# Two bank reads ahead of the last lower half, and one lower half made by GpSimd in place of VectorE

## The chip, the cores and the metric

The kernel runs on one core of a Trainium2 chip. The metric is the device time of one execution in microseconds (us), as a median of several runs. The core has five engines with queues of their own that meet only at semaphores: TensorE (PE in the profile, its weight loads PEld), VectorE (DVE), ScalarE (ACT), GpSimd (POOL) and SyncE (SP), which issues the loads.

## The reference

Two transformer-like blocks on one sequence of 512 tokens, width 1024, all in float32. The change touches only the feed-forward part of the first block:

```python
h = rmsnorm(x, norm_ffn[l])
x = x + jnp.square(jax.nn.relu(h @ w_ff1[l])) @ w_ff2[l]   # 1024 -> 4096 -> 1024
```

## The kernel before

Each float32 operand of TensorE is split into an upper half (rounded to fp32r by ScalarE, `w_hi`, `f_hi`) and a lower half (the remainder, `w_lo`, `f_lo`). A product is then three matmuls: upper by upper, upper by lower and lower by upper. Weights come through a ring of four slots in `raw`, `w_hi` and `w_lo`, each 128 x 1024; a slot is a panel.

The feed-forward part runs in four quarters of the hidden width (`ffn(i)`, 1024 hidden columns each). A quarter has eight dense panels (`h @ w_ff1`), and then four **pairs** (`pair(i, c)`, c = 0 to 3), which multiply the squared activations by `w_ff2`. A pair makes two output tiles of 128 rows by 512 tokens with seven products in place of eight (Strassen's scheme in Winograd's form). The seven are called p1 to p7. Each is one **turn** of TensorE: twelve matmuls of 256 columns into one half of a bank. The first pair of a quarter takes the turns in the order p1, p5, p2, p6, p3, p7, p4 (`FIRST_PAIR`), the others in the order p1, p2, p6, p5, p7, p3, p4 (`NEXT_PAIR`).

The weights of a pair fill the four slots. Slot 0 is a loaded panel, used by p1 and p2. Slots 1 and 2 hold four sums and differences of the loaded panels (`ss`), which VectorE makes (`first` to `fourth` in `weight_sums`); p6 and p5 use the halves of slot 1, p7 and p3 those of slot 2. Slot 3 is half a loaded panel, for p4. ScalarE makes the upper halves of slots 0 to 3 in this order (`pair_upper`). Before the change the lower halves are made as follows:

- slot 0 by GpSimd, four pieces of 128 x 256 (`pair_lower`, through the helper at L830);
- slot 1 by VectorE, two instructions of 128 x 512 (`lower(0)` for p6, `lower(1)` for p5, L2466), counted by `sum_lo_dve`;
- slot 2 by GpSimd, four pieces, counted by `sum_lo_pool`;
- slot 3 by GpSimd, two pieces.

GpSimd goes through the pairs in this order. A pair's p1 needs all of slot 0, its upper half and its lower half (`panel_split`).

After a turn VectorE adds its bank to `xT` (a **bank read**, L2557 or, for the first p1, L2519). A later turn in the same bank half goes on from what stands there, so it must wait until the earlier one has been read. Turns wait for reads by the count of `chain`, five per pair (`read(n)`). In the first pair p3 waits for the read of p5, and p7 for that of p6. VectorE is also forming the activations of the last hidden tile then (`forms(7)`, with `f_lo` for the lower halves, the newest of them at L2510).

In the last quarter ScalarE and VectorE also begin the two normalizations that follow: `scale_upper`, `scale_lower`, the squares (`both_squares(e)`, L1808 and L1809) and their sums (`add_squares(e)`, into `hf`).

## Time and profile before

| | |
|---|---|
| median of 3 runs | 1632.52 us (1631.73 to 1632.7) |
| the profiled execution: its own time | 1632.63 us |
| its span, first to last instruction | 1630.9 us |
| TensorE busy | 1603.0 us, 98% |
| GpSimd busy in the four pairs of the second quarter | 36.48 of 40.13 us |
| VectorE busy in the same stretch | 29.92 of 40.13 us |

The profile is of one execution. Its span is 1.7 us shorter than the execution's own time, which includes what lies before the first and after the last instruction. Busy shares over the whole span say little here, since the pairs take 40 us in each of four quarters. In a row of the timeline the columns are the start and the length in us, engine, line, operation, output and inputs, and in brackets the idle time before it with what ended it.

### The profile page before, as it was taken

Reading aid. Unit: us, or ns where it says so; the run is one execution under the profiler, and the core shown is the slowest. Engines: PE = TensorE matmul, PEld = TensorE weight load, DVE = VectorE, ACT = ScalarE, POOL = GpSimd, SP = SyncE. Lnnn points to the kernel's source line nnn. Section 1 sums busy time; section 2 is a strip of 40 time slices with the busy share of each in tenths; the row PEclk is TensorE's granted clock in tenths of the full one; section 3 lists DMA queues with packets and bytes.
Section 4 is the critical chain, followed back from the end, with each engine's and each line's share of the span. In section 5 each row is a group of like instructions: output and inputs, shape, how many; then the busy total and the mean of one; then the engine's idle time right before and its main releaser. Section 6 shows DMA issues by size and latency. Waiting matters only on the chain.

```text
span 1630.9 us, 23121 instructions
## 1 busy us (share of the span) xinstructions
PE 1603.0 (98%) x8079; PEld 1349.4 (83%) x8079; DVE 1001.6 (61%) x1563; ACT 874.9 (54%) x1189; POOL 777.2 (48%) x966
## 2 busy tenths in 40 slices
PE   7999999999999999999999999999999999999998
PEld 6888888888888898989897788888888887888886
DVE  3466666631114676758587957447447548688677
ACT  6467777753234544444466645444444446755675
POOL 7453333346656495867679535635635633000000
PEclk9999999999999999999999999999999999999999
DMA  7222221123333233242424222422422423332321
GB/s 210 78 79 63 64 77 58 46 65 116 91 109 98 78 95 112 78 116 79 128 65 118 76 66 78 116 65 78 116 65 66 116 64 93 92 93 68 107 63 62
DMA packets 249053, 143.00 MB, mean 88 GB/s; under 512 B 6161, under 2 KB 245522, under 8 KB 248978
## 3 DMA queue, kind: packets, MB, share of 16 engines
q1 hardware_dynamic: 248978, 142.00, 30.4%
q8 instruction: 46, 0.75, 0.2%
q14 instruction: 29, 0.24, 0.0%
HBM read 139.89 MB, written 2.10 MB: 87 GB/s over the span
## 4 chain that ended last, share of the span: by engine, by line
PE 75%; DVE 2%; issue 1%; POOL 1%; ACT 0%; DVEq 0%
PE bank L897 17%; PE bank L898 17%; PE bank L905 17%; PE bank L1163 3%; PE bank L1168 2%; PE bank L1166 2%; PE bank L888 1%; PE bank L890 1%; PE bank L889 1%; PE bank L1291 1%; PE bank L1272 1%; PE bank L1274 1%; PE bank L1273 1%; PE bank L1417 1%; PE bank L1418 1%
## 5 line engine op out<-in xcount | busy, mean ns | idle before, releaser
L830 POOL TENSOR_TENSOR w_lo<-raw,w_hi 128x256 fp32r<-128x256 f32 x864 | 704.9, 849 | 551.9 <-ACT w_hi L1524 521.3
L897 PE MATMUL bank<-h_hi,w_hi 128*128 128x512 f32 x1252 | 497.1, 397 | 0.0
L898 PE MATMUL bank<-h_lo,w_hi 128*128 128x512 f32 x1252 | 487.9, 390 | 0.0
L1524 ACT ACTIVATE w_hi<-raw 128x1024 fp32r<-128x1024 f32 x232 | 243.5, 1054 | 317.5 <-PE bank L905 263.8
L905 PE MATMUL bank<-h_hi,w_lo 128*128 128x512 f32 x1252 | 309.8, 389 | 0.0
L897 PEld LDWEIGHTS bank<-h_hi,w_hi 128*128 128x128 f32 x1252 | 235.1, 188 | 54.1 <-issue 6.0
L898 PEld LDWEIGHTS bank<-h_lo,w_hi 128*128 128x128 f32 x1252 | 235.1, 188 | 52.0 <-issue 4.1
L905 PEld LDWEIGHTS bank<-h_hi,w_lo 128*128 128x128 f32 x1252 | 235.0, 188 | 49.2 <-issue 0.5
L1163 PE MATMUL bank<-f_hi,w_hi 128*128 128x256 f32 x448 | 127.7, 285 | 6.4 <-DVE xT L2557 5.3
L1166 PE MATMUL bank<-f_lo,w_hi 128*128 128x256 f32 x448 | 126.7, 283 | 0.0
L1168 PE MATMUL bank<-f_hi,w_lo 128*128 128x256 f32 x448 | 126.7, 283 | 0.0
L2421 DVE TENSOR_TENSOR xT<-xT,bank 128x512 f32<-128x512 f32 x70 | 45.5, 684 | 88.1 <-PE bank L905 53.2
L1163 PEld LDWEIGHTS bank<-f_hi,w_hi 128*128 128x128 f32 x448 | 85.8, 192 | 8.3 <-issue 8.0
L1166 PEld LDWEIGHTS bank<-f_lo,w_hi 128*128 128x128 f32 x448 | 85.9, 192 | 0.2
L1168 PEld LDWEIGHTS bank<-f_hi,w_lo 128*128 128x128 f32 x448 | 85.9, 192 | 0.0
L830 POOL TENSOR_TENSOR w_lo<-ss,w_hi 128x256 fp32r<-128x256 f32 x64 | 61.7, 994 | 31.6 <-ACT w_hi L1753 31.3
L2405 DVE TENSOR_TENSOR gated<-sg,bank 128x512 f32<-128x512 f32 x16 | 11.0, 688 | 104.6 <-PE bank L905 104.3
L2557 DVE TENSOR_TENSOR xT<-xT,bank 128x256 f32<-128x256 f32 x112 | 46.3, 419 | 38.8 <-PE bank L1168 37.8
L2871 DVE TENSOR_TENSOR w_lo<-raw,w_hi 128x1024 fp32r<-128x1024 f32 x40 | 48.6, 1217 | 0.0
L1624 ACT ACTIVATE ee<-ee 128x512 f32<-128x512 f32 (+1 forms) x56 | 33.6, 613 | 27.8 <-DVE ee L2276 22.2
L1029 PE MATMUL bank<-qk 128*128 128x64 f32 (+1 forms) x384 | 42.4, 265 | 0.0
L1029 PEld LDWEIGHTS bank<-qk 128*128 128x128 f32 (+1 forms) x384 | 41.7, 183 | 0.8 <-DVE hf L2366 0.3
(465 smaller groups left out, 2852.5 us busy)
## 6 DMA issues: line engine op xcount, KB each, us to landing
raw<-in_w_ff SPq DMA_DIRECT2D x64, 512.0 KB, 4.1
raw<-in_w_in SPq DMA_DIRECT2D x56, 512.0 KB, 3.7
raw<-in_m_w_in SPq DMA_DIRECT2D x48, 512.0 KB, 3.9
raw<-in_r_w_in SPq DMA_DIRECT2D x24, 512.0 KB, 3.9
raw<-in_m_w_out SPq DMA_DIRECT2D x16, 512.0 KB, 3.4
raw<-in_r_w_out SPq DMA_DIRECT2D x16, 384.0 KB, 3.1
raw<-in_w_up_b SPq DMA_DIRECT2D x8, 512.0 KB, 4.1
raw<-in_w_out SPq DMA_DIRECT2D x8, 512.0 KB, 4.1
```

Source lines behind the costliest of these rows:

```text
L830: return pool.tensor_tensor(w_lo[:, s, part], full, w_hi[:, s, part].bitcast(F32), ALU.subtract)
L897: pe.matmul(dst, w_hi[:, s, c], hi[:, k, :], start=(k == 0), stop=False)
L898: pe.matmul(dst, w_hi[:, s, c], lo[:, k, :], start=False, stop=False)
L905: mm = pe.matmul(dst, w_lo[:, s, c], hi[:, k, :], start=False, stop=(k == kt - 1))
L1029: mm = pe.matmul(dst.rearrange("p (b t) -> p b t", t=h), qk[:, m - 2, c], right, start=True, stop=True, skip_group_check=True)
L1163: pe.matmul(dst, w_hi[:, s, at], f_hi[:, form, k, :], start=(k == 0 and (name in ("p1", "p2", "p5") or r == 2)), stop=False, skip_group_ch ...
L1166: pe.matmul(dst, w_hi[:, s, at], f_lo[:, form, k, :], start=False, stop=False, skip_group_check=True)
L1168: mm = pe.matmul(dst, w_lo[:, s, at], f_hi[:, form, k, :], start=False, stop=(k == NC - 1), skip_group_check=True)
L1524: act.activation(w_hi[:, p % RING, :], raw[:, p % RING, :], ACT.Copy).then_inc(hi_ready[p % RING], 1)
L2421: dve.tensor_tensor(xT[:, j, :], xT[:, j, :], bank[t % RING][:], ALU.add).then_inc(taken[t % RING], 1)
L2557: ins = dve.tensor_tensor(x, x, src[:, left], op)
L2871: dve.tensor_tensor(w_lo[:, q, :], raw[:, q, :], w_hi[:, q, :].bitcast(F32), ALU.subtract).then_inc(lo_ready[q], 1)
```

## The change

Three things change, all in the pairs.

1. The lower half of slot 1 that p5 uses is made by GpSimd, in two pieces of 128 x 256 between slot 0 and slot 2, and no more by VectorE. `sum_lo_pool` counts three to a pair instead of two, `sum_lo_dve` one.
2. In the first pair of a quarter VectorE reads the bank of p5 (`second_read`) ahead of the newest activation's last lower half, and reads p6 ahead of p2. The counts that p7 and p4 wait for follow.
3. In the last quarter ScalarE squares tiles 2 and 3 after the third pair and not after the second, and tile 4 after the fourth and not after the third.

```diff
@@ pair_lower (GpSimd)
                 ins.then_inc(lo_ready[one], 1)
+                pool.wait_ge(sum_hi, i * (2 * NC) + (2 * c + 1))
+                for q in range(2):
+                    part = slice(S + q * QP, S + (q + 1) * QP)
+                    ins = lower(1, part, ss[:, c % 2, 1, q * QP:(q + 1) * QP])
+                ins.then_inc(sum_lo_pool, 1)
                 pool.wait_ge(sum_hi, i * (2 * NC) + (2 * c + 2))
@@ pair (TensorE)
...
                     elif name == "p5":
                         bank_ready(t + 2, i, F_N)
-                        pe.wait_ge(sum_lo_dve, i * (2 * NC) + (2 * c + 2))
+                        pe.wait_ge(sum_lo_pool, i * (3 * NC) + (3 * c + 1))
                     elif name == "p7":
-                        pe.wait_ge(sum_lo_pool, i * (2 * NC) + (2 * c + 1))
-                        read(3 if c else 4)
+                        pe.wait_ge(sum_lo_pool, i * (3 * NC) + (3 * c + 2))
+                        read(3)
...
                     elif name == "p4":
                         panel_split(pe, p + 1, i, F_N)
-                        read(5 if c else 3)
+                        read(5 if c else 4)
@@ ffn (ScalarE)
-                        for e in [(0, 1), (2, 3), (4,), (5, 6, 7)][c]:
+                        for e in [(0, 1), (), (2, 3), (4, 5, 6, 7)][c]:
                             both_squares(e)
@@ forms (VectorE)
                            .then_inc(ft_made, 1)
+                        if c == NC - 1:
+                            second_read()
                         dve.wait_ge(fthi_made, i * (3 * NC) + (3 * c + 3))
...
+                def second_read():
+                    dve.wait_ge(turn_done, i * (FORMS * NC) + turn_at(0, "p5"))
+                    dve.tensor_tensor(xT[:, 1, HALF:S], xT[:, 1, HALF:S], bank[2][:, 0:HALF], ALU.add)\
                        .then_inc(chain, 1)
@@ ffn (VectorE)
                     if e == 6:
                         lower(0)
-                        lower(1)
...
-                        elif lower and n < 6:
-                            lower(n - 4)
+                        elif lower and n == 4:
+                            lower(0)
...
                     if c == 0:
-                        reads[0] = 1
-                        add("p5", x2[:, right], r2, ALU.add)
+                        reads[0] = 2
+                        add("p6", x1[:, right], r1, ALU.add)
                         add("p2", x1[:, left], r3, ALU.add, before=1)
                         behind(2)
-                        add("p6", x1[:, right], r1, ALU.add)
+                        add("p3", x1[:, right], r2, ALU.add, taken[2 + c % 2], before=3)
                         behind(3)
-                        add("p3", x1[:, right], r2, ALU.add, taken[2 + c % 2], before=4)
...
```

GpSimd's queue in a pair, before: slot 0 (`raw`), slot 2 (`ss`), slot 3, and then slot 0 of the next pair.

```order
L830 TENSOR_TENSOR w_lo<-raw,w_hi 128x256 x3
L847 ISA
L830 TENSOR_TENSOR w_lo<-ss,w_hi 128x256 [waits sum_hi]
L830 TENSOR_TENSOR w_lo<-ss,w_hi 128x256 x3
L830 TENSOR_TENSOR w_lo<-raw,w_hi 128x256 [waits hi_ready1]
L830 TENSOR_TENSOR w_lo<-raw,w_hi 128x256
L830 TENSOR_TENSOR w_lo<-raw,w_hi 128x256 [waits hi_ready2]
L830 TENSOR_TENSOR w_lo<-raw,w_hi 128x256 x3
```

The same place after the change:

```order
L830 TENSOR_TENSOR w_lo<-raw,w_hi 128x256 x3
L847 ISA
L830 TENSOR_TENSOR w_lo<-ss,w_hi 128x256 [waits sum_hi]
L830 TENSOR_TENSOR w_lo<-ss,w_hi 128x256
L852 REGISTER_ALU
L830 TENSOR_TENSOR w_lo<-ss,w_hi 128x256 [waits sum_hi]
L830 TENSOR_TENSOR w_lo<-ss,w_hi 128x256 x3
L830 TENSOR_TENSOR w_lo<-raw,w_hi 128x256 [waits hi_ready1]
L830 TENSOR_TENSOR w_lo<-raw,w_hi 128x256
L830 TENSOR_TENSOR w_lo<-raw,w_hi 128x256 [waits hi_ready2]
L830 TENSOR_TENSOR w_lo<-raw,w_hi 128x256 x3
```

Two pieces on `ss` have come in ahead of the four, with a wait of their own on `sum_hi`; ten pieces to a pair have become twelve.

VectorE's queue from the forms of the last hidden tile through the first pair, before (`xT<-xT,bank` are the bank reads of p5, p2, p6, p3, p7 and p7, `ss` the sums for the next pair, `w_lo` is `lower(0)`):

```order
L2507 TENSOR_TENSOR ft<-ff,ft 128x256 [waits ft_made]
L2510 TENSOR_TENSOR f_lo<-ft,f_hi 128x2x256 [waits fthi_made]
L2557 TENSOR_TENSOR xT<-xT,bank 128x256 [waits turn_done]
L2557 TENSOR_TENSOR xT<-xT,bank 128x256 [waits turn_done,chain]
L2457 TENSOR_TENSOR ss<-ss,raw 128x512 [waits s_made]
L2557 TENSOR_TENSOR xT<-xT,bank 128x256 [waits turn_done]
L2461 TENSOR_TENSOR ss<-raw,ss 128x512 [waits s_made]
L2557 TENSOR_TENSOR xT<-xT,bank 128x256 [waits turn_done,chain]
L2557 TENSOR_TENSOR xT<-xT,bank 128x256 [waits turn_done]
L2557 TENSOR_TENSOR xT<-xT,bank 128x256 [waits turn_done,chain]
L2466 TENSOR_TENSOR w_lo<-ss,w_hi 128x512 [waits sum_hi]
```

The same place after the change:

```order
L2512 TENSOR_TENSOR ft<-ff,ft 128x256 [waits ft_made]
L2531 TENSOR_TENSOR xT<-xT,bank 128x256 [waits turn_done]
L2517 TENSOR_TENSOR f_lo<-ft,f_hi 128x2x256 [waits fthi_made]
L2568 TENSOR_TENSOR xT<-xT,bank 128x256 [waits turn_done]
L2568 TENSOR_TENSOR xT<-xT,bank 128x256 [waits turn_done,chain]
L2462 TENSOR_TENSOR ss<-ss,raw 128x512 [waits s_made]
L2568 TENSOR_TENSOR xT<-xT,bank 128x256 [waits turn_done,chain]
L2466 TENSOR_TENSOR ss<-raw,ss 128x512 [waits s_made]
L2568 TENSOR_TENSOR xT<-xT,bank 128x256 [waits turn_done]
L2568 TENSOR_TENSOR xT<-xT,bank 128x256 [waits turn_done,chain]
L2471 TENSOR_TENSOR w_lo<-ss,w_hi 128x512 [waits sum_hi]
```

The read of p5 (now L2531) stands ahead of `f_lo`, and that of p6 ahead of the sums.

ScalarE's queue in the last quarter, between the third and the fourth pair, before (the squares are those of tile 4):

```order
L1756 ACTIVATE w_hi<-raw 128x512 [waits raw_full3,turn_done]
L1527 ACTIVATE h_hi<-xT,cols 128x512 [waits taken2]
L1527 ACTIVATE h_hi<-xT,cols 128x512 [waits taken0]
L1808 ACTIVATE sq<-xT 128x512 [waits sq2_used]
L1809 ACTIVATE sq<-xT,cols 128x512
L1524 ACTIVATE w_hi<-raw 128x1024 [waits turn_done,panel_done0,raw_full0]
```

And after (the squares are those of tiles 2 and 3):

```order
L1761 ACTIVATE w_hi<-raw 128x512 [waits raw_full3,turn_done]
L1532 ACTIVATE h_hi<-xT,cols 128x512 [waits taken2]
L1532 ACTIVATE h_hi<-xT,cols 128x512 [waits taken0]
L1813 ACTIVATE sq<-xT 128x512 [waits sq2_used]
L1814 ACTIVATE sq<-xT,cols 128x512
L1813 ACTIVATE ff<-xT 128x512 [waits sq2_used]
L1814 ACTIVATE ff<-xT,cols 128x512
L1529 ACTIVATE w_hi<-raw 128x1024 [waits turn_done,panel_done0,raw_full0]
```

VectorE's `add_squares(2)` stands, before and after, right behind the third pair's read of p4 and ahead of the fourth pair's read of p1, and it needs the squares of tile 2.

## Rows read from the trace of the kernel before

**Rows 1.** The page, busy time, share of the span and instructions of each engine.

```profile
PE 1603.0 (98%) x8079; PEld 1349.4 (83%) x8079; DVE 1001.6 (61%) x1563; ACT 874.9 (54%) x1189; POOL 777.2 (48%) x966
```

**Rows 2.** Waits of TensorE: line, releaser, us in total, times, longest us.

```profile
PE bank L1163 <- DVE xT L2557: 5.3, 7, 1.2
...
PE bank L1163 <- POOL w_lo L830: 0.9, 1, 0.9
```

**Rows 3.** Timeline of TensorE, second quarter, first matmuls of some turns.

```profile
655.47 0.28 PE L1163 MATMUL bank<-f_hi,w_hi 128*128 128x256 f32 x1
...
662.63 0.36 PE L1163 MATMUL bank<-f_hi,w_hi 128*128 128x256 f32 x1 [1.17 <-DVE xT L2557]
...
664.58 0.38 PE L1163 MATMUL bank<-f_hi,w_hi 128*128 128x256 f32 x1 [0.28 <-DVE xT L2557]
...
667.54 0.28 PE L1163 MATMUL bank<-f_hi,w_hi 128*128 128x256 f32 x1
...
677.62 0.28 PE L1163 MATMUL bank<-f_hi,w_hi 128*128 128x256 f32 x1
```

**Rows 4.** Timeline of VectorE, second quarter, first pair.

```profile
657.34 0.73 DVE L2495 TENSOR_TENSOR ft<-ff,ft 128x256 f32<-128x256 f32 x1
657.99 1.22 DVE L2498 TENSOR_TENSOR f_lo<-ff,f_hi 128x512 fp32r<-128x512 f32 x1
...
661.46 0.69 DVE L2510 TENSOR_TENSOR f_lo<-ft,f_hi 128x512 fp32r<-128x512 f32 x1 [0.70 <-ACT f_hi L1781]
662.07 0.74 DVE L2557 TENSOR_TENSOR xT<-xT,bank 128x256 f32<-128x256 f32 x2
...
666.97 0.73 DVE L2466 TENSOR_TENSOR w_lo<-ss,w_hi 128x512 fp32r<-128x512 f32 x1
```

**Rows 5.** Timeline of ScalarE, second quarter, first pair.

```profile
651.19 1.04 ACT L1750 ACTIVATE w_hi<-ss 128x1024 fp32r<-128x1024 f32 x1
...
660.80 0.63 ACT L1781 ACTIVATE f_hi<-ft 128x512 fp32r<-128x512 f32 x1 [2.28 <-DVE ft L2507]
661.34 0.61 ACT L1756 ACTIVATE w_hi<-raw 128x512 fp32r<-128x512 f32 x1
661.86 1.04 ACT L1747 ACTIVATE w_hi<-raw 128x1024 fp32r<-128x1024 f32 x1
```

**Rows 6.** Timeline of GpSimd, second quarter.

```profile
655.35 4.46 POOL L830 TENSOR_TENSOR w_lo<-ss,w_hi 128x256 fp32r<-128x256 f32 x4 [7.00 <-ACT w_hi L1753]
662.03 5.12 POOL L830 TENSOR_TENSOR w_lo<-raw,w_hi 128x256 fp32r<-128x256 f32 x6 [2.22 <-ACT w_hi L1756]
667.52 3.79 POOL L830 TENSOR_TENSOR w_lo<-ss,w_hi 128x256 fp32r<-128x256 f32 x4 [0.37 <-ACT w_hi L1753]
671.26 6.12 POOL L830 TENSOR_TENSOR w_lo<-raw,w_hi 128x256 fp32r<-128x256 f32 x6
...
687.68 2.84 POOL L830 TENSOR_TENSOR w_lo<-ss,w_hi 128x256 fp32r<-128x256 f32 x4 [0.62 <-ACT w_hi L1753]
```

**Rows 7.** Timeline of VectorE, second quarter, instructions with two inputs in SBUF.

```profile
654.70 1.29 DVE L2466 TENSOR_TENSOR w_lo<-ss,w_hi 128x512 fp32r<-128x512 f32 x2
...
668.08 0.78 DVE L2466 TENSOR_TENSOR w_lo<-ss,w_hi 128x512 fp32r<-128x512 f32 x1
...
675.28 0.80 DVE L2466 TENSOR_TENSOR w_lo<-ss,w_hi 128x512 fp32r<-128x512 f32 x1
```

**Rows 8.** Timeline of TensorE, last quarter, p4 of the third pair and p1 of the fourth.

```profile
857.82 0.28 PE L1163 MATMUL bank<-f_hi,w_hi 128*128 128x256 f32 x1
...
860.31 0.36 PE L1163 MATMUL bank<-f_hi,w_hi 128*128 128x256 f32 x1 [0.89 <-POOL w_lo L830]
```

**Rows 9.** Timelines of GpSimd, ScalarE and VectorE, last quarter, around the fourth pair's start.

```profile
854.05 6.12 POOL L830 TENSOR_TENSOR w_lo<-raw,w_hi 128x256 fp32r<-128x256 f32 x6
...
861.82 0.71 ACT L1809 ACTIVATE sq<-xT,cols 128x512 f32<-128x512 f32 x1
...
859.86 1.38 DVE L2542 TENSOR_TENSOR hf<-hf,sq 128x1024 f32<-128x1024 f32 x1
```

More of the change, by code:

```diff
@@ L1144, in pair @@
                     elif name == "p6":
-                        pe.wait_ge(sum_lo_dve, i * (2 * NC) + (2 * c + 1))
+                        pe.wait_ge(sum_lo_dve, i * NC + (c + 1))
                         read(1)
@@ L1148, in pair @@
                         bank_ready(t + 2, i, F_N)
-                        pe.wait_ge(sum_lo_dve, i * (2 * NC) + (2 * c + 2))
+                        pe.wait_ge(sum_lo_pool, i * (3 * NC) + (3 * c + 1))
                     elif name == "p7":
-                        pe.wait_ge(sum_lo_pool, i * (2 * NC) + (2 * c + 1))
-                        read(3 if c else 4)
+                        pe.wait_ge(sum_lo_pool, i * (3 * NC) + (3 * c + 2))
+                        read(3)
                     elif name == "p3":
-                        pe.wait_ge(sum_lo_pool, i * (2 * NC) + (2 * c + 2))
+                        pe.wait_ge(sum_lo_pool, i * (3 * NC) + (3 * c + 3))
                         read(4 if c else 2)
@@ L2448, in first @@
                     if c > 1 or not isinstance(i, int) or i > 0:
-                        dve.wait_ge(sum_lo_pool, i * (2 * NC) + (2 * c - 2))
+                        dve.wait_ge(sum_lo_pool, i * (3 * NC) + (3 * c - 3))
                     dve.tensor_tensor(to[:, 1, :], two[:, 0:S], two[:, S:2 * S], ALU.add).then_inc(s_made, 1)
@@ L2519, in first_read @@
                     dve.tensor_tensor(xT[:, 0, 0:HALF], xT[:, 0, 0:HALF], bank[0][:, 0:HALF], ALU.add)\
+                       .then_inc(chain, 1)
+                def second_read():
+                    dve.wait_ge(turn_done, i * (FORMS * NC) + turn_at(0, "p5"))
+                    dve.tensor_tensor(xT[:, 1, HALF:S], xT[:, 1, HALF:S], bank[2][:, 0:HALF], ALU.add)\
                        .then_inc(chain, 1)
```

## Prediction

> **What bounds the kernel now.** The page comes first: TensorE is busy for 98% of the span [rows 1], so a change gains only where TensorE waits. The list of its waits comes next. Nearly all of what the pairs lose stands in two entries: seven waits on VectorE's bank reads, 5.3 us together, and one of 0.9 us on GpSimd's lower halves [rows 2]. The second quarter (the pairs that begin at 655.47) shows the pattern; the others repeat it within some tenths, and I treat the four alike. In its first pair TensorE loses 1.17 us ahead of p3, which waits for the read of p5, and 0.28 us ahead of p7, which waits for that of p6 [rows 3]. From p1 of the first pair to p1 of the second it takes 667.54 - 655.47 = 12.07 us, from there to the third pair 677.62 - 667.54 = 10.08 us [rows 3]. In that second interval nothing is lost, so 10.08 us is a pair's own length, 1.44 us to a turn, and the first pair loses 1.99 us.
>
> Why are the reads late? VectorE reads p5 only at 662.07, right behind the `f_lo` at 661.46, which had waited for ScalarE's `f_hi` at 660.80 [rows 4, 5]. The bank had long been full.
>
> The third view is GpSimd's queue. From 662.03 on it has almost no idle time: 0.37 us before 667.52, none before 671.26 [rows 6]. Ten pieces, from 667.52 to 671.26 + 6.12 = 677.38, take 9.86 us, and p1 of the third pair, which needs the last of them, starts at 677.62. So a second engine stands just below the bound, with some 0.1 to 0.4 us to spare per pair.
>
> **The change, part by part.** *The reads.* VectorE has done the last `ft` by 660.80, where ScalarE takes it up [rows 5]. The read of p5 fits into the gap until 661.46 [rows 4] at no cost, and ends some 0.45 us later. Without a wait p3 is due at 655.47 + 4 x 1.44 = 661.23, so its stall goes. The read of p6 takes the place at 662.07, where p5's stood, and ends before 662.5; p7 is due at 661.23 + 1.44 = 662.67. That stall goes too, and p1 of the second pair is due at 655.47 + 10.08 = 665.55.
>
> *Where that stall goes.* This p1 needs slot 0's lower half. GpSimd makes it as the last four of the six pieces that start at 662.03 and end at 667.15 [rows 6]. It can't start sooner: it waits for ScalarE's L1756, which is queued behind the `f_hi` at 660.80, and this waits for VectorE's `ft` [rows 5]. Nothing of that chain is moved by the change. In the last quarter's trace p1 starts 0.14 us after GpSimd's last piece (854.05 + 6.12 = 860.17, then 860.31) [rows 8, 9]. So p1 starts at 667.15 + 0.15 = 667.30 at best, against 667.54: of the 1.99 us, 0.24 is gained.
>
> *What a piece costs.* Four pieces with VectorE idle or reading banks take 2.84 us, the last of them 0.74, so 0.70 us each in a row [rows 6]. The ten in 9.86 us should take 7.04, and 2.82 are lost. In that stretch six VectorE instructions with both inputs in SBUF run beside them (from 668.08 to 675.28 [rows 7]; two `lower` and four sums), so one costs GpSimd 0.47 us; I call it a hit. The Trainium skill (SBUF - State Buffer, "Who interferes with whom") states that a VectorE instruction with two SBUF inputs and a GpSimd instruction that reads SBUF exclude each other, the second blocking until the first is done. By that rule a hit would be VectorE's whole instruction; what it gives is the last rival below.
>
> *Slot 1's half on GpSimd.* In the first pair it costs nothing on the path: ScalarE has the upper half by 652.23 [rows 5], and GpSimd idles for 7.00 us until 655.35 [rows 6]. In the others it adds 2 x 0.70 = 1.40 us and takes away one hit (`lower(1)`), so a pair takes 12 x 0.70 + 5 x 0.47 = 10.75 us of GpSimd against 10.08 of TensorE. GpSimd becomes the bound of these pairs.
>
> *`lower(0)` comes sooner.* With p7 read early, VectorE makes the second pair's `lower(0)` at about 665.7 instead of 666.97 [rows 4]. There it hits a piece of slot 0, where before it mostly met GpSimd's gap: +0.47.
>
> *The sum for a quarter*, as p1's start after minus before: second pair 667.15 + 0.47 + 0.15 - 667.54 = +0.23. Third pair: + (10.75 - 10.08) = +0.90. Fourth pair: +1.57. In the fourth pair the rest of GpSimd's work has room again (VectorE makes no sums there, and pieces cost 0.70), so 1.57 stays. Four quarters: 6.3 us.
>
> *The squares.* VectorE's `add_squares(2)` now waits for squares that ScalarE makes after the third pair. Before, ScalarE was through with the first tile's squares there at 861.82 + 0.71 = 862.53, that is 4.71 us after p4's start at 857.82 [rows 8, 9]. The fourth p1 started 2.49 us after that p4, and starts 2.49 + 0.67 = 3.16 us after it now. So the sum begins 1.55 us into the fourth pair, takes 1.38 us [rows 9], and the read of p1 (0.42 with its latency 0.15 to TensorE) ends 3.5 us into it. p6 waits for that read and is due at 2.88: 0.6 us, once. Behind it on VectorE stand the other reads, which catch up inside their turns. The two squares that moved to the end wait, as the later ones did, on the chain of sums, and cost nothing more.
>
> Sum: 6.3 + 0.6 = +6.9 us on the profiled execution's 1632.63 us, 1639.5. The median of the three runs is 0.1 lower, so I take 1639.4.
>
> *Bounds.* Hits: 8 intervals with 5 of them, 40 in all. At the least 0.25 each (about half of what the stretch shows, since a piece may be hit only in part); then twelve pieces take 8.40 + 1.25 = 9.65 us, less than a pair, the 1.57 shrinks to 0.0 and only the 0.6 of the squares is left, 1633.1. At most the whole uncovered instruction, 1.29 - 0.69 = 0.60 us from one start to the next [rows 4, 7], which adds 40 x 0.13 = 5.2. The first pair: GpSimd's pieces also slow VectorE's forms there (0.73 against some 0.42 us for the 256-wide `ft`, 1.22 against 0.69 for the 512-wide `f_lo` [rows 4]). Pieces that move away could shorten that chain by up to 0.8 us a quarter, the two new ones in front could lengthen it by as much: -3.2 to +3.2. `lower(0)`'s hit: 0 to 0.47 a quarter, so -1.9 to 0. I take the middle rows, since GpSimd has no gap in which a hit would be lost.
>
> **The rivals.**
>
> *GpSimd keeps up, faster.* If slot 0 of the second pair were ready at 665.4 and twelve pieces fitted into 10.08 us, each quarter would gain 1.99, less 0.6 once: 1632.6 - 7.4 = 1625.2. For it speaks that only seven reads are named as releasers in the list [rows 2]; against it the ends of GpSimd's pieces, 667.15 and 677.38, each within 0.4 us of the turn that needs them [rows 3, 6]. It decides at the start of the six pieces: they would have to start 1.7 us before 662.03. Chance 0.07.
>
> *No change.* The first pair's chain gets 0.8 us shorter, `lower(0)` falls into a gap (0.47), and the two intervals cost 0.67 each as above: per quarter 1.57 - 1.27 = 0.3, with the squares +1.8 us, 1634.4. What speaks for it is that VectorE loses an instruction of 0.60 us just ahead of that chain; against it that the read of the last dense tile behind it waits for TensorE, not for VectorE's time. Chance 0.20.
>
> *Slower as summed.* 1636 to 1643, chance 0.60.
>
> *Slower by whole blocking.* With 0.60 us to a hit: 6.9 + 5.2 = +12.1, 1644.7. Against it stands the 0.47 of the row, which that rule would have as 0.60. By the rule of the skill's SBUF page this would be the likely one; the trace so far doesn't bear out its full size. Chance 0.13.
>
> **How the numbers follow.** This kernel's runs spread by 0.06%, and I take 0.2%, 3.3 us, as the least that can be told. Slower by more than that: 0.60 + 0.13 = 0.73, less 0.02 for sums near the edge, 0.71. Within it: 0.20 + 0.02 = 0.22. Faster: 0.07. The range of 8 in 10 goes from the lower bound of the hits to the upper, 1633.1 to 1644.7, and leaves out the fast rival and what lies beyond whole blocking. The likeliest case alone: 1636 to 1643.
>
> **What would show it.** In the profile after, the waits of p3 and p7 on bank reads should be gone, and in their place the p1 of the second, third and fourth pairs should wait for `w_lo` of GpSimd, 1.5 to 2 us in the second and 0.6 to 0.7 in each of the others. GpSimd should run without a gap from the first pair's slot 3 to the fourth pair's p1, in stretches of twelve pieces of about 10.75 us. In the last quarter p6 of the fourth pair should wait about 0.6 us for VectorE. The prediction is wrong if GpSimd's stretches stay near 10.1 us, if slot 0 of the second pair is ready by 666 on this time scale, or if p1 is not what waits.

## The result and the profile after

The changed kernel takes 1642.09 us (median of 4 runs, 1642.07 to 1643.28) against 1632.12 us of the kernel before (4 runs, 1631.57 to 1632.7). The ratio is 1.0063, with a 95% interval of 1.0051 to 1.0075: slower by 10.0 us, where +6.9 was predicted. 1642.1 lies inside the range and inside the likeliest case. The predicted mechanism is there. A second one, not foreseen, hides part of it and adds a loss of its own; with the second taken away the same kernel loses 7.05 us (e10 below).

The profiled execution took 1642.08 us, its span is 1640.3 us, 9.4 more than before. The page of the changed kernel, as [rows 1], and the two entries of its list of TensorE's waits that answer to [rows 2]:

```profile
PE 1608.0 (98%) x8079; PEld 1354.9 (83%) x8079; DVE 995.5 (61%) x1547; ACT 874.7 (53%) x1189; POOL 795.1 (48%) x998
```

```profile
PE bank L1168 <- POOL w_lo L830: 9.1, 7, 2.0
PE bank L1168 <- DVE xT L2568: 1.8, 1, 1.8
```

The waits of p3 and p7 are gone, as predicted: none of the seven waits on bank reads is left, and the one now listed, of p6 in the last pair, is new. In their place stand seven on GpSimd. But the two entries add up to 10.9 us against 6.2 before, only 4.7 more. The rest of the loss is in no list of waits: TensorE's busy time has grown by 5.0 us with the same 8079 matmuls. Its timeline in the second, third and last quarter shows how:

```profile
669.03 0.36 PE L1168 MATMUL bank<-f_hi,w_hi 128*128 128x256 f32 x1 [1.98 <-POOL w_lo L830]
...
670.18 0.28 PE L1168 MATMUL bank<-f_hi,w_hi 128*128 128x256 f32 x1
670.30 0.28 PE L1171 MATMUL bank<-f_lo,w_hi 128*128 128x256 f32 x1
...
670.56 0.42 PE L1168 MATMUL bank<-f_hi,w_hi 128*128 128x256 f32 x1
670.77 0.42 PE L1171 MATMUL bank<-f_lo,w_hi 128*128 128x256 f32 x1
...
673.77 0.35 PE L1168 MATMUL bank<-f_hi,w_hi 128*128 128x256 f32 x1
...
756.79 0.35 PE L1168 MATMUL bank<-f_hi,w_hi 128*128 128x256 f32 x1 [1.98 <-POOL w_lo L830]
...
767.32 0.39 PE L1168 MATMUL bank<-f_hi,w_hi 128*128 128x256 f32 x1 [0.23 <-POOL w_lo L830]
...
778.10 0.35 PE L1168 MATMUL bank<-f_hi,w_hi 128*128 128x256 f32 x1 [0.44 <-POOL w_lo L830]
...
866.44 0.36 PE L1168 MATMUL bank<-f_hi,w_hi 128*128 128x256 f32 x1 [0.44 <-POOL w_lo L830]
...
871.34 0.35 PE L1168 MATMUL bank<-f_hi,w_hi 128*128 128x256 f32 x1 [1.80 <-DVE xT L2568]
```

Rows with 1.98 are p1 of the second pair. Behind the one of the second quarter, matmuls follow 0.12 us apart (670.18 to 670.30), and then, from 670.56 to 673.77, 15 of them 0.21 us apart. Those 15 take 3.21 us where 15 x 0.12 = 1.80 would do. With the edges this costs 1.5 us. The windows view of the same kernel names it (columns: stretch, its length, busy time and instructions of TensorE, its weight loads, VectorE, ScalarE, GpSimd, then the granted clock, DMA share and GB/s):

```profile
669.03:680.67 11.64, 11.64 (x85) 11.64 (x86) 7.25 (x11) 3.18 (x3) 11.64 (x14) 0.85 0.32 95
756.79:767.32 10.53, 10.30 (x84) 10.10 (x85) 7.03 (x12) 3.37 (x4) 10.53 (x13) 1.00 0.33 100
767.32:778.10 10.78, 10.34 (x85) 10.17 (x85) 7.34 (x13) 4.03 (x5) 10.78 (x13) 1.00 0.34 97
871.34:875.30 3.96, 3.96 (x21) 3.96 (x22) 2.94 (x5) 0.00 (x0) 3.96 (x5) 0.57 0.07 15
...
670.78:674.20 3.42, 3.42 (x19) 3.42 (x19) 2.23 (x4) 0.76 (x1) 3.42 (x6) 0.54 0.42 125
```

The second pair of the second quarter ran at a mean granted clock of 0.85, with TensorE busy all the time; the same pair of the third quarter, behind the same wait, at 1.00. The start of the last pair's p6 ran at 0.57. The last line takes in the slow matmuls and hardly more, and has 0.54: they are at the lower of the two levels, half of full speed, 1.2 GHz. The Trainium skill (TensorE: Matmul & The Clock Gate, "Wait — 56ns, not 53.3ns?") has matmuls follow each other by their columns over 1.2 GHz at that level, which is an estimated 0.213 us for 256 columns; the rows' 0.21 agrees. I call such a stretch a **fall**. This profile has four in the pairs, each of 15 or 16 matmuls: in the second pair of the first, second and last quarter, and in the last pair.

GpSimd's queue in the second and the third quarter, as [rows 6]:

```profile
663.23 5.65 POOL L830 TENSOR_TENSOR w_lo<-raw,w_hi 128x256 fp32r<-128x256 f32 x6 [2.22 <-ACT w_hi L1761]
668.85 4.63 POOL L830 TENSOR_TENSOR w_lo<-ss,w_hi 128x256 fp32r<-128x256 f32 x6
673.44 5.57 POOL L830 TENSOR_TENSOR w_lo<-raw,w_hi 128x256 fp32r<-128x256 f32 x6
...
756.61 5.12 POOL L830 TENSOR_TENSOR w_lo<-ss,w_hi 128x256 fp32r<-128x256 f32 x6
761.69 5.57 POOL L830 TENSOR_TENSOR w_lo<-raw,w_hi 128x256 fp32r<-128x256 f32 x6
767.22 5.12 POOL L830 TENSOR_TENSOR w_lo<-ss,w_hi 128x256 fp32r<-128x256 f32 x6
772.32 5.63 POOL L830 TENSOR_TENSOR w_lo<-raw,w_hi 128x256 fp32r<-128x256 f32 x6
777.91 1.43 POOL L830 TENSOR_TENSOR w_lo<-ss,w_hi 128x256 fp32r<-128x256 f32 x2
```

It runs without a gap, as predicted. In the third quarter twelve pieces take 767.22 - 756.61 = 10.61 us and 777.91 - 767.22 = 10.69 us, where 10.75 was predicted, and p1 of the third and fourth pair start right behind them (767.32, 778.10). That is (10.61 - 8.40) / 5 = 0.44 and (10.69 - 8.40) / 5 = 0.46 us to a hit, against the predicted 0.47. In the second quarter, with the fall, twelve take 10.2 us (668.85 to 673.44 + 5.57 = 679.01) and end 1.7 us before p1 of the third pair, at 680.67. There TensorE was the later one.

From p1 to p1 the pairs took (us; predicted: before + 0.23, + 0.67, + 0.67; the last column is a run described below):

| quarter | before | predicted | after | after with filler (e10) |
|---|---|---|---|---|
| first | 11.74, 10.11, 10.15 | 11.97, 10.78, 10.82 | 12.32, 11.63, 10.08 | 12.35, 10.68, 10.69 |
| second | 12.07, 10.08, 10.08 | 12.30, 10.75, 10.75 | 12.41, 11.64, 10.08 | 12.44, 10.53, 10.78 |
| third | 12.07, 10.08, 10.08 | 12.30, 10.75, 10.75 | 12.41, 10.53, 10.78 | 12.45, 10.53, 10.78 |
| last | 11.91, 10.08, 11.13 | 12.14, 10.75, 11.80 | 12.35, 11.62, 10.69 | 12.38, 10.60, 11.75 |

Together the four quarters lose 7.0 us, the last pair 3.5 more (from its p1 to the first matmul behind it: 870.45 - 860.31 = 10.14 before, 880.09 - 866.44 = 13.65 after). The sum is 10.5. In these two executions the first quarter's first p1 began 0.9 us earlier after than before (568.96 against 569.85), ahead of anything the change touches, so 9.6 remain.

### The profile page after: what moved, and what is told of

The parts are those of the page before. It is cut to its first block, busy times and chain, and to the rows that moved or that the text cites. A ratio compares the mean times of both kernels' runs of the same rounds, so it can differ in the third digit from the quotient of the medians.

```text
span 1640.3 us, 23177 instructions
## 1 busy us (share of the span) xinstructions
PE 1608.0 (98%) x8079; PEld 1354.9 (83%) x8079; DVE 995.5 (61%) x1547; ACT 874.7 (53%) x1189; POOL 795.1 (48%) x998
## 4 chain that ended last, share of the span: by engine, by line
PE 71%; DVE 3%; issue 3%; POOL 2%; ACT 1%; DVEq 0%; ACTq 0%
PE bank L902 16%; PE bank L903 16%; PE bank L910 16%; PE bank L1168 2%; PE bank L1171 2%; PE bank L1173 2%; POOL w_lo L830 2%; PE bank L893 1%; PE bank L895 1%; PE bank L894 1%; PE bank L1296 1%; PE bank L1277 1%; PE bank L1279 1%; PE bank L1278 1%; PE bank L1422 1%
## 5 line engine op out<-in xcount | busy, mean ns | idle before, releaser
L1168 PE MATMUL bank<-f_hi,w_hi 128*128 128x256 f32 x448 | 130.8, 292 | 10.9 <-POOL w_lo L830 9.1
L830 POOL TENSOR_TENSOR w_lo<-ss,w_hi 128x256 fp32r<-128x256 f32 x96 | 82.0, 887 | 22.9 <-ACT w_hi L1755 15.9
```

The source lines that it names most:

```text
L830: return pool.tensor_tensor(w_lo[:, s, part], full, w_hi[:, s, part].bitcast(F32), ALU.subtract)
L1168: pe.matmul(dst, w_hi[:, s, at], f_hi[:, form, k, :], start=(k == 0 and (name in ("p1", "p2", "p5") or r == 2)), stop=False, skip_group_ch ...
```

## The experiments

Theory A is the prediction's chain (GpSimd, with two more pieces and more hits, sets when p1 starts), together with the fall, which the trace after showed. Its rivals (B) are named with each run. All times are compared with the kernel before on the same chip.

| run | median us | before us | ratio, 95% interval |
|---|---|---|---|
| e1, reads only | 1639.78 | 1631.87 | 1.0049, 1.0032 to 1.0066 |
| e2, GpSimd's half only | 1640.39 | 1631.87 | 1.0048, 1.0031 to 1.0064 |
| e3, squares only | 1633.73 | 1631.87 | 1.0009, 1.0000 to 1.0019 |
| e4, all but the squares | 1639.98 | 1631.87 | 1.0052, 1.0035 to 1.0068 |
| e5, reads, newest upper half sooner | 1631.56 | 1632.20 | 0.9996, 0.9987 to 1.0006 |
| e6, e5 with GpSimd's half | 1636.35 | 1632.20 | 1.0022, 1.0013 to 1.0032 |
| e8, e1 with filler | 1635.52 | 1632.20 | 1.0020, 1.0010 to 1.0029 |
| e9, newest upper half sooner, alone | 1641.47 | 1632.20 | 1.0054, 1.0037 to 1.0070 |
| e10, after with filler | 1639.91 | 1632.86 | 1.0045, 1.0028 to 1.0061 |
| e11, e5 with the read of p5 still sooner | 1633.91 | 1632.86 | 1.0005, 0.9996 to 1.0015 |
| e12, e11 with GpSimd's half in two pairs | 1641.02 | 1632.86 | 1.0047, 1.0030 to 1.0064 |

**e1, the reads alone.** Before, with part 2 of the change and nothing else.

```diff
+                        if c == NC - 1:
+                            second_read()
                         dve.wait_ge(fthi_made, i * (3 * NC) + (3 * c + 3))
```

> Only the reads move: p5's and p6's bank reads stand where the changed kernel has them, both lower halves of slot 1 stay on VectorE, the squares stay. Theory A (the first pair's stalls move to one place): p3 and p7 no longer wait, p1 of the second pair waits some 2.0 us for GpSimd's slot 0 in one piece, and behind so long a wait the granted clock falls to 1.2 GHz for some 17 matmuls (0.21 us from one to the next in place of 0.12), 1.5 us; the pair starts gain and lose nothing else, since GpSimd has ten pieces. Per quarter +0.2 and +1.5 in the quarters where the clock falls: +5 to +7 us in all if it falls in three or four. Rival B (all that is lost is GpSimd's two extra pieces and the squares, the reads themselves gain or are neutral): -1 to +1 us, no half-rate stretch.

It takes 7.9 us more. Waits of p3 and p7 are gone, and p1 of the second pair waits 2.4 us in every quarter. The entry of the waits, then p1 of the second quarter's second pair and the windows of that pair in the second and the third quarter:

```profile
PE bank L1163 <- POOL w_lo L830: 10.2, 5, 2.4
```

```profile
670.53 0.36 PE L1163 MATMUL bank<-f_hi,w_hi 128*128 128x256 f32 x1 [2.43 <-POOL w_lo L830]
```

```profile
670.53:682.15 11.62, 11.62 (x85) 11.62 (x85) 7.09 (x12) 3.18 (x3) 8.22 (x11) 0.85 0.37 102
758.66:768.80 10.14, 10.14 (x84) 10.14 (x85) 7.45 (x12) 3.19 (x3) 9.11 (x11) 1.00 0.35 103
```

And GpSimd's six pieces ahead of that p1:

```profile
664.28 6.10 POOL L830 TENSOR_TENSOR w_lo<-raw,w_hi 128x256 fp32r<-128x256 f32 x6 [2.22 <-ACT w_hi L1756]
```

So moving the reads gains nothing, even where GpSimd has no more to do: two waits of 1.2 and 0.3 us become one of 2.4. Slot 0's lower half starts no sooner, and takes 6.10 us instead of 5.12 [rows 6], the price of two hits: `lower(0)` and `lower(1)` both come sooner now and fall on it. And one wait in place of two brings the fall (first, second and last quarter, 1.5 us each), which the two did not bring before. It came a little above what was expected.

**e2, GpSimd's half alone.** Before, with part 1 only.

```diff
                 ins.then_inc(lo_ready[one], 1)
+                pool.wait_ge(sum_hi, i * (2 * NC) + (2 * c + 1))
+                for q in range(2):
+                    part = slice(S + q * QP, S + (q + 1) * QP)
+                    ins = lower(1, part, ss[:, c % 2, 1, q * QP:(q + 1) * QP])
+                ins.then_inc(sum_lo_pool, 1)
```

> Only the lower half for p5 goes to GpSimd, reads and squares stay as before. Theory A: the waits of p3 (1.2) and p7 (0.3) stay, so the wait of p1 in the second pair is short and the clock stays at 2.4 GHz; GpSimd's twelve pieces take 10.6 to 10.8 us in the second and third pair against 10.08, p1 of the third and fourth pair wait 0.4 to 0.7 each: +1.2 to +1.6 us per quarter, +5 to +6.5 in all. Rival B (the extra pieces by themselves bring the long wait and the half rate): p1 of the second pair waits over 1.5 us, half-rate stretches show, +8 or more. Rival C (GpSimd has room for them): -0.5 to +1.

It takes 8.5 us more, over what was expected (runs from 1638.16 to 1641.59). TensorE's waits for slot 0, third pair of the second quarter and fourth pair of the last:

```profile
680.99 0.38 PE L1168 MATMUL bank<-f_hi,w_hi 128*128 128x256 f32 x1 [0.49 <-POOL w_lo L830]
...
868.24 0.55 PE L1168 MATMUL bank<-f_hi,w_hi 128*128 128x256 f32 x1 [2.40 <-POOL w_lo L830]
```

The first is Theory A's: intervals of 10.73 and 10.77 us in the second and third quarter instead of 10.08, and no fall there: p1 waits a little in each pair and never long. The second is what was missed: in the last quarter p1 of the fourth pair waited 0.89 us already before [rows 8], GpSimd's lag of two pairs comes on top of it, and behind 2.40 us the clock falls. The lag alone is not all of it: both of VectorE's 1024-wide sums of squares (at 855.45 and 866.29) run beside the twelve pieces ahead of that p1, which take 12.64 us (855.41 to 868.05). In e10 below, where the second sum comes only behind p1, they take 11.65 us and p1 waits 1.41.

**e3, the squares alone.** Before, with part 3 only.

```diff
-                        for e in [(0, 1), (2, 3), (4,), (5, 6, 7)][c]:
+                        for e in [(0, 1), (), (2, 3), (4, 5, 6, 7)][c]:
```

> Only the squares of tiles 2, 3 and 4 move, all else as before. Theory A: VectorE's sum of squares behind the third pair waits for ScalarE until 4.7 us after p4's start, and the read of p1 of the fourth pair stands behind it; p1 starts 2.5 us after p4's start, so p6 waits 2.2 + 1.7 + 0.4 + 0.15 - 2.9 = 1.6 us for the read, +1.6, or +3.1 if the clock falls to 1.2 GHz behind that wait. Rival B (p6's wait in the changed kernel came of GpSimd's lag, not of the squares): within 0.5 us of before, no wait of p6 in the fourth pair.

It takes 1.9 us more (10 runs; the interval of the ratio reaches down to no change). The last pair takes 11.46 us instead of 10.14, 1.3 more where 1.6 was expected: p6 of the last pair waits for VectorE's read of p1, which stands behind the sum of the squares; no fall follows:

```profile
864.62 0.36 PE L1163 MATMUL bank<-f_hi,w_hi 128*128 128x256 f32 x1 [1.10 <-DVE xT L2557]
```

**e4, the change without the squares.** After, with `[(0, 1), (2, 3), (4,), (5, 6, 7)][c]`.

> The changed kernel with the squares back where they were. Theory A: p6 of the last quarter's fourth pair no longer waits 2.0 us nor runs at 1.2 GHz behind it, the rest is as in the changed kernel: 3.5 us less than that, +6 to +7 over before. Rival B (the lag before the fourth pair would make p6 wait anyway): as the changed kernel, +10.

It takes 8.1 us more, above the 6 to 7 expected. What Theory A said of p6 held: its wait and the fall behind it are gone, and the last pair takes 10.15 us instead of 13.65. The third quarter repeats the one of the changed kernel (12.41, 10.53, 10.78), and this time the second does so too: falls come in the first and last quarter only, though p1 of the second pair starts as late in all four. The same program part at the same place falls in one execution and not in another. By e1, e2 and e3 each part loses alone (7.9, 8.5, and for the squares 1.9, hardly clear of noise); the sum of the three, 18.3, is well above the 10.0 of all together, in part because the fall that the reads bring hides GpSimd's lag.

**e8 and e10, filler.** If the fall is the missing part, matmuls that nobody reads, put where TensorE would stand still, should take it away. Twelve of them, into a bank that is free, stand ahead of the second pair's p1, in e8 on e1, in e10 on the changed kernel. They are extra work; no part of the computation is left out.

```diff
                     if name == "p1":
+                        if c == 1:
+                            for _ in range(12):
+                                pe.matmul(bank[7][:, 0:HALF], f_hi[:, 0, 0, 0:P], f_hi[:, 0, 0, :], start=True,
+                                          stop=True, skip_group_check=True)
                         bank_ready(t, i, F_N)
```

> The reads-only kernel with twelve matmuls of 256 columns, whose result nobody reads, ahead of the second pair's p1, where TensorE waits 2.4 us for GpSimd. They fill some 1.4 us of that wait and add no work behind it. Theory A (the 1.5 us behind the long wait come of the clock that falls to 1.2 GHz after TensorE has stood still for 2.4 us): no stretch of matmuls 0.21 us apart behind that p1; the wait itself stays, so p1 starts as in the reads-only kernel and the second pair takes 10.1 instead of 11.6 us: +3 to +4.5 over before, 3.5 to 4.5 less than reads only. Rival B (the slow stretch comes of operands that arrive late, or of something else in that pair): the stretch stays, +8 as reads only, or more.

> The whole changed kernel with the twelve filler matmuls ahead of the second pair's p1. Theory A (of the changed kernel's loss, the half-rate stretches behind the long wait are one part and GpSimd's twelve pieces another, and the first hides the second where it comes): no half-rate stretch behind the second pair's p1 in any quarter, and in every quarter the third and fourth p1 wait for GpSimd, 0.45 and 0.6 to 0.7 us, where the changed kernel showed that in one quarter only; with 0.3 to 0.6 in the first pair 1.4 to 1.8 us per quarter, +6 to +7, and p6 of the last quarter waits 0.6 to 1.2 us: +6.5 to +8 in all. Rival B (the third and fourth pair lose nothing, all is the slow clock): +2 to +4.

e8 is 4.3 us faster than e1 by the medians, 1635.52 against 1639.78 (4.6 by what each adds to the kernel before on its chip, 3.3 against 7.9). In its second quarter the filler and p1:

```profile
665.98 1.60 PE L1144 MATMUL bank<-f_hi 128*128 128x256 f32 x12
668.57 0.36 PE L1167 MATMUL bank<-f_hi,w_hi 128*128 128x256 f32 x1 [1.00 <-POOL w_lo L830]
```

p1 starts as late as in e1 (intervals of 12.66 to 12.81 us), but no fall is left, and the second pairs take 10.14 or 10.15 us, as the one of e1's third quarter, which had no fall. Three falls of 1.5 us each, as e1's profile has them, are 4.5: that the half rate comes of the wait is shown, and its price.

e10 takes 7.05 us more than before. Without a fall GpSimd's lag can be seen in all four quarters (table above): waits of slot 0 in each pair, GpSimd's stretches unchanged.

```profile
PE bank L1172 <- POOL w_lo L830: 6.1, 12, 1.4
```

```profile
669.47 5.12 POOL L830 TENSOR_TENSOR w_lo<-ss,w_hi 128x256 fp32r<-128x256 f32 x6
674.56 5.58 POOL L830 TENSOR_TENSOR w_lo<-raw,w_hi 128x256 fp32r<-128x256 f32 x6
680.10 5.11 POOL L830 TENSOR_TENSOR w_lo<-ss,w_hi 128x256 fp32r<-128x256 f32 x6
```

From 669.47 to 680.10 twelve pieces take 10.63 us. The four quarters lose 1.72, 1.52, 1.53 and 1.61, 6.4 us (6.3 predicted), and p6 of the last pair idles for 0.41 us and makes that pair 0.64 longer (10.78 against 10.14; 0.6 predicted).

**e5 and e6, the newest upper half sooner.** The first pair's chain goes over ScalarE, so here its newest `f_hi` stands behind the second pair's slot 0 instead of ahead of it, and slot 0 can be ready sooner; VectorE reads p6 right behind p5. e5 has e1's reads and no more work for GpSimd, e6 has GpSimd's half too.

```diff
                 act.activation(w_hi[:, 0, :], raw[:, p % RING, :], ACT.Copy).then_inc(hi_ready[p % RING], 1)
+                if behind:
+                    behind()
...
-                        pair_upper(i, c + 1)
+                        pair_upper(i, c + 1, behind=(lambda: newest(NC - 1)) if c == 0 else None)
```

> As the reads-only kernel, and ScalarE makes the upper halves of slot 3 and of the next pair's slot 0 ahead of the newest activation's last upper half, in the 2.3 us in which it idled there, so that GpSimd starts on them some 1.5 us sooner; p6's read stands ahead of the newest f_lo too. Both lower halves of slot 1 stay on VectorE. Theory A (GpSimd's slot 0, late because of ScalarE's queue, is what the reads were traded for): p1 of the second pair finds slot 0 ready or nearly, no stall over 0.5 us in the first two pairs, the clock stays at 2.4 GHz, a gain of 1.5 to 1.9 us per quarter, -6 to -7.5 in all. Rival B (p1 of the second pair waits for something else, or GpSimd's pieces fill the time anyway): a wait of over 1.5 us stays before that p1, within 1.5 us of the reads-only kernel, +6 to +9.

> As the run before, but with the lower half for p5 on GpSimd as in the changed kernel (squares as in the kernel before). Theory A: no wait before the second pair's p1, but GpSimd's twelve pieces still take 10.7 us a pair, so the third and fourth p1 wait 0.5 to 0.7 us: -0.3 to -0.8 us per quarter, -1 to -3 in all; worse than the run before by 4 to 5 us. Rival B (the half on GpSimd costs nothing once GpSimd starts in time): -6 to -7.5, as the run before.

e5 equals the kernel before (0.9996, 0.9987 to 1.0006) where 6 us and more were expected: that expectation failed. The first pair does gain 0.84 us (11.23 against 12.07), and then it is given back. It gains no more because p3 still waits 0.86 us for the read of p5: GpSimd's pieces, now earlier, run beside VectorE's last two forms, which take 0.96 and 0.95 us instead of 0.41 each. GpSimd in the second quarter, then p1 of the third pair:

```profile
658.98 5.65 POOL L830 TENSOR_TENSOR w_lo<-raw,w_hi 128x256 fp32r<-128x256 f32 x6
666.36 4.26 POOL L830 TENSOR_TENSOR w_lo<-ss,w_hi 128x256 fp32r<-128x256 f32 x4 [1.73 <-ACT w_hi L1755]
670.58 6.01 POOL L830 TENSOR_TENSOR w_lo<-raw,w_hi 128x256 fp32r<-128x256 f32 x6
```

```profile
676.64 0.39 PE L1163 MATMUL bank<-f_hi,w_hi 128*128 128x256 f32 x1 [0.49 <-POOL w_lo L830]
```

Slot 0 is early, but slot 2's upper half is not: GpSimd idles for 1.73 us, and from 666.36 its ten pieces take until 670.58 + 6.01 = 676.59, with p1 right behind. So even ten pieces leave GpSimd no time to make good a late start. e6 takes 4.15 us more than before where 1 to 3 less was expected, so it failed too. It is 4.8 us slower than e5, inside the 4 to 5 of Theory A, but by luck: the two more pieces cost only some 0.5 us in each of the first three quarters, and 3.3 us come in the last, with a wait of 2.39 us and a fall as in e2.

**e9, that move alone.** Before, with the `f_hi` behind slot 0, reads in the old order.

> The kernel before, with only ScalarE's early upper halves of slot 3 and slot 0; reads, slot 1 and squares as before. Theory A: p3 and p7 of the first pair still wait for reads that stand behind the newest f_lo, which comes some 0.5 us later now: the first pair's waits stay at 1.5 to 2.0 us, 0 to +2 us in all; the gain needs both edits. Rival B (GpSimd's earlier start alone is worth the gain): -3 or less.

It takes 9.3 us more, a miss. GpSimd, started sooner, runs six pieces from 661.51 on beside VectorE's last two forms, which take 0.96 us each instead of 0.41. So ScalarE's `f_hi` comes 1.1 us later after the first p1 than before, and the reads, which queue on VectorE behind the `f_lo` that needs it, 1.5 us later. p3 of the first pair:

```profile
665.88 0.43 PE L1163 MATMUL bank<-f_hi,w_hi 128*128 128x256 f32 x1 [2.65 <-DVE xT L2563]
```

One wait of 2.65 us on VectorE, and the clock falls behind it in three of four quarters (first pairs of 13.24, 14.56, 14.54, 14.53 us). So the fall does not need a wait for GpSimd.

**e11 and e12.** e11 is e5 with the read of p5 right behind that of p1; e12 adds GpSimd's half in the first two pairs alone, where GpSimd idles before slot 2.

```diff
                         if c == NC - 1:
                             first_read()
+                            second_read()
```

```diff
+                if c < 2:
+                    pool.wait_ge(sum_hi, i * (2 * NC) + (2 * c + 1))
...
```

> As the kernel with reads and early upper halves, but p5's read stands right behind p1's, ahead of the forms that GpSimd's pieces slow down. Theory A: p3 no longer waits (1.0 us less per first pair), then GpSimd's ten pieces from slot 2's upper half on are the bound of the second pair, 0.5 to 0.8 us of wait before the third pair's p1 and 0.1 to 0.3 before the fourth: first pair 10.1 to 10.4 us against 12.0, -1.0 to -1.5 us per quarter, -4 to -6 in all. Rival B (GpSimd's chain gives all of it back): within 1 us of before.

> As the run before, and GpSimd makes the lower half for p5 in the first two pairs alone, where it idles ahead of slot 2 (7 us, and 1.5 to 2 us), VectorE in the other two. Theory A: the half costs nothing there and takes one hit off the stretch that follows; the third pair's p1 waits 0.2 to 0.5 us less than in the run before: -5 to -7.5 in all. Rival B (slot 2's pieces start later by the half): no better than the run before, or worse by 0.5 us per quarter.

Both went the rival's way, and e12 went further: it is 7.1 us slower than e11, where the rival named up to 0.5 per quarter. In e11 the first pair is down to 10.90 us, 1.2 less than before, and the third pair's p1 gives back 1.5 (second pair 11.54 us). GpSimd's idle time ahead of slot 2 and its cause on ScalarE:

```profile
668.74 4.18 POOL L830 TENSOR_TENSOR w_lo<-ss,w_hi 128x256 fp32r<-128x256 f32 x4 [2.67 <-ACT w_hi L1755]
```

```profile
666.65 1.06 ACT L1752 ACTIVATE w_hi<-ss 128x1024 fp32r<-128x1024 f32 x1 [2.35 <-DVE ss L2463]
```

ScalarE waits there for VectorE's sums: the next late link. In e12 the half fills part of that gap (1.72 us are left) and pushes slot 2's pieces back; p1 of the third pair waits 1.74 us and more, and the clock falls in all four quarters.

```profile
680.07 0.38 PE L1172 MATMUL bank<-f_hi,w_hi 128*128 128x256 f32 x1 [1.75 <-POOL w_lo L830]
```

No version was measurably faster than the kernel before.

## Why the prediction was right, and where it was not

*The reads.* That the stall goes held for p3 and p7, in every quarter. The read of p5 stands at 661.89 in the second quarter, ahead of `f_lo`.

*Where the stall goes.* "This p1 needs slot 0's lower half" held. The six pieces start 6.61 us after the first p1 (669.03 - 12.41 = 656.62, 663.23) where it was 6.56 before: "nothing of that chain is moved" is right in sum, though VectorE's forms did lengthen, as the bound allowed. `lower(0)` came sooner and fell on slot 0. In the timeline of VectorE, as [rows 4]:

```profile
653.68 1.07 DVE L2455 TENSOR_TENSOR ss<-raw 128x512 f32<-128x512 f32 x1
654.67 0.96 DVE L2490 TENSOR_TENSOR ft<-ff 128x256 f32<-128x256 f32 x1
...
661.89 0.41 DVE L2531 TENSOR_TENSOR xT<-xT,bank 128x256 f32<-128x256 f32 x1
...
666.36 1.26 DVE L2471 TENSOR_TENSOR w_lo<-ss,w_hi 128x512 fp32r<-128x512 f32 x1
```

The six pieces took 5.65 us instead of 5.12, 0.53 against the 0.47 predicted. The term "+0.23" was mis-sized where the quarters differ: 0.34 in the second and third, 0.58 and 0.44 in the first and last, whose first pairs were shorter before (11.74 and 11.91). "I treat the four alike" cost 0.8 us here (1.7 in all, 0.9 predicted).

*What a piece costs, and twelve of them.* Right: 10.61 and 10.69 us against 10.75. The bound of whole blocking, 0.60 to a hit, is not borne out; hits took 0.44 to 0.46. The rule of the Trainium skill (SBUF - State Buffer, "Who interferes with whom"), by which the second of the two is blocked for the whole instruction, would have made it an estimated 11.4 us to twelve pieces (8.40 and five whole instructions of 0.60). So the rule, as the prediction read it, has the direction right here, and its size about a third too high.

*The intervals.* The sum of the second and third intervals is right, 5.3 us (1.45, 1.56, 1.15, 1.10) against 5.4. But in the first, second and last quarter it is right by chance: there the fall took 1.5 us in the second pair, and GpSimd's lag of twice some 0.6 was hidden behind it. Of the changed kernel's quarters only the third shows the predicted step by itself; all four of e10 do. As idle time the waits are shorter than the "0.6 to 0.7" named: 0.23 and 0.44 us in the third quarter, where the intervals grew by 0.45 and 0.70.

*The squares: the term that was mis-sized.* The "0.6 us, once" became 3.5 us. The rows of ScalarE and VectorE in the last pair, as [rows 9], the last bank read the one that p6 waits for:

```profile
868.32 0.71 ACT L1814 ACTIVATE sq<-xT,cols 128x512 f32<-128x512 f32 x1
```

```profile
869.06 1.80 DVE L2553 TENSOR_TENSOR hf<-hf,sq 128x1024 f32<-128x1024 f32 x1 [2.54 <-ACT sq L1814]
870.78 0.41 DVE L2568 TENSOR_TENSOR xT<-xT,bank 128x256 f32<-128x256 f32 x1
```

The sum starts 869.06 - 866.44 = 2.62 us into the pair where 1.55 was reckoned, because the fall had hidden GpSimd's lag and p1 no longer came late (interval 10.69 instead of 11.80). It took 1.80 instead of 1.38, beside GpSimd's pieces. So p6 started 871.34 - 866.44 = 4.90 us into the pair instead of 2.88, 2.0 late, and its own wait brought a fall, 1.5. In e10, with no fall ahead of it, the step comes out as written: p6 starts 870.34 - 866.83 = 3.51 us into the pair, where 3.5 was reckoned.

*The step that was missing.* The prediction reckoned a wait as its length alone. It foresaw a wait of "1.5 to 2 us" ahead of the second pair's p1, and did not ask what one long wait does that two short ones (1.17 and 0.28 [rows 3]) do not. Four falls of 1.5 us are 6.0 in the profiled execution. Up to the fourth p1 three of them lie in the pairs, 4.5 us, and yet those quarters lose only 0.6 more than e10's: for the other 3.9 us TensorE would have waited for GpSimd anyway. In the last pair the cost is 2.9 (3.51 against 0.64): p6 starts 1.4 later, and the fourth fall adds 1.5. So in the profiled pairs the falls are worth 3.5 net; by the medians it is the difference of the changed kernel's and e10's additions to the kernel before, 10.0 - 7.05 = 2.9 us. With that the prediction's 6.9 and the measured 10.0 nearly meet.

*Still open.* Why the clock falls behind one wait and not behind another of the same length. In the profiles' pairs 18 of 23 waits of 1.7 to 2.7 us were followed by a fall, and none of those of 1.4 or less. The five without are the 1.98 us of the third quarter, e1's 2.43 there, e4's 1.98 in the second and third and e9's 2.59 in the first. The Trainium skill (TensorE: Matmul & The Clock Gate, "What's actually happening") says that the chip's look at TensorE's activity runs on freely, unaligned with the kernel. The traces agree as far as they go: in e12 the granted clock drops at 592.01, 680.75, 769.50 and 858.25 us, 88.75 us apart within a hundredth, while the waits ahead of it ended 0.15, 0.68, 1.22 and 0.84 us sooner, so the drops keep a beat that is not the kernel's. That this is what tells equal waits apart stays argued, since no run here moved a wait along the time axis on purpose. Whether another order of GpSimd's queue (slot 0 ahead of slot 2) would gain was not tried.

## What to carry to other kernels

When a read is moved ahead, look for what the next turn waits on: here another engine's queue stood 0.2 to 0.4 us behind the stall that was removed, and taking over a second engine's work there made it the bound. Price a wait by what TensorE does behind it, too: here waits up to 1.4 us cost their length, and most of those of 1.7 us and more cost about 1.5 us on top, so gathering short waits into a long one can lose. Filler matmuls tell the two parts of the price apart. Work that an engine does "in a gap" is free only if what stands behind it in that queue isn't what the next turn needs (e6, e12).

## What the runs showed of the hardware that was not expected

- One wait of some 2 us, in a kernel whose TensorE is busy for 98% of the span, can bring the granted clock to 1.2 GHz for some 15 or 16 matmuls of 256 columns (3.2 to 3.4 us), and did so in 18 of 23 cases; it costs about 1.5 us where nothing else waits. Twelve filler matmuls (1.60 us) in the wait ahead of the second pair's p1 prevented it in all eight cases (e8, e10); without them the same waits brought it in six of eight (e1 and the changed kernel).
- VectorE and GpSimd slow each other. Beside the new pieces VectorE's 256-wide `ft` (654.67) took 0.96 us and its 512-wide sum (653.68) 1.07. The same two instructions in the kernel before, with GpSimd idle there [rows 6], took 0.42 and 0.68:

```profile
652.53 0.68 DVE L2450 TENSOR_TENSOR ss<-raw 128x512 f32<-128x512 f32 x1
653.45 0.42 DVE L2485 TENSOR_TENSOR ft<-ff 128x256 f32<-128x256 f32 x1 [0.24 <-ACT ff L1770]
```

`lower(0)` took 1.26, against 0.73 in [rows 4]. Not every instruction beside a piece gets longer: the sum at 663.94, in the midst of GpSimd's six pieces, took 0.69.
